# Sparse attention in eight pipelined groups of heads, and delta scan interleaved with stick attention

## The reference, cut to what matters

```python
q, k, v, g, beta = (chunk(t) for t in (q, k, v, g, beta))
...
v_new = u_c - jnp.einsum('bhcd,bhde->bhce', w_c, state)
o = jnp.einsum('bhcd,bhde->bhce', qd, state) + jnp.einsum('bhcs,bhse->bhce', qk_c, v_new)
...
log_rem = jnp.where(causal, jax.nn.log_sigmoid(-z), 0.0)
after = lax.cumsum(log_rem, axis=3, reverse=True) - log_rem
attn = jnp.where(causal, jnp.exp(jax.nn.log_sigmoid(z) + after), 0.0)
```

```python
p = _masked_softmax(logits, mask)
...
o = gates[..., 0:1] * o_cmp + gates[..., 1:2] * o_slc + gates[..., 2:3] * o_win
```

## Time and profile before

| | us |
|---|---|
| median of 3 runs | 3720.51 |
| lowest, highest | 3718.89, 3734.4 |
| profiled execution | 3725.97 |
| its span | 3724.2 |
| its mean granted TensorE clock | 0.921 |

### The profile page before, as it was taken

The page is one execution under the profiler, slowest core; times in us unless marked ns, Lnnn a source line. Parts: engine busy times, 40 slices in busy tenths (PEclk is TensorE's granted clock), DMA queues, the critical chain, the costliest instruction groups (busy, mean ns, idle before and its releaser), DMA issues. The chain is left out here.

```text
span 3724.2 us, 51371 instructions
## 1 busy us (share of the span) xinstructions
PE 3272.8 (88%) x20778; PEld 2927.4 (79%) x20778; DVE 2336.0 (63%) x2592; ACT 1543.3 (41%) x1455; POOL 186.3 (5%) x134
## 2 busy tenths in 40 slices
PE   6998699999877789999999999995489989966599
PEld 6987589999866678788788887894279989953599
DVE  7974258846742388888888885796834315434444
ACT  3432133335321177677677774441033204401243
POOL 0012000000210000000000000001600000000000
PEclk9999799989998899999999999997789969985799
DMA  7630168734201189999999996351045424520153
GB/s 314 240 113 1 46 224 325 275 125 169 80 1 68 45 297 361 343 369 364 336 365 368 367 365 260 136 184 64 0 148 187 162 68 158 184 76 0 46 181 135
DMA packets 130378, 703.20 MB, mean 189 GB/s; under 512 B 11009, under 2 KB 16145, under 8 KB 74385
## 3 DMA queue, kind: packets, MB, share of 16 engines
q1 hardware_dynamic: 118384, 650.30, 47.7%
q0 software_dynamic: 6368, 47.19, 3.2%
q10 hardware_dynamic: 5440, 3.17, 0.3%
HBM read 698.50 MB, written 1.07 MB: 188 GB/s over the span
## 5 line engine op out<-in xcount | busy, mean ns | idle before, releaser
L1048 DVE TENSOR_TENSOR ring_low<-ring,parts 128x2048 fp32r<-128x2048 f32 x570 | 1298.1, 2288 | 397.1 <-ACT parts L1911 366.0
L429 PE MATMUL banks<-parts 128*128 128x256 f32 (+1 forms) x3712 | 1170.5, 315 | 42.2 <-DVE tail_parts L1048 25.5
L430 PE MATMUL banks<-tail_parts,parts 128*128 128x256 f32 x3744 | 1062.5, 284 | 0.0
L1911 ACT ACTIVATE parts<-ring 128x2048 fp32r<-128x2048 f32 x234 | 448.4, 1917 | 876.7 <-PE banks L431 726.8
L431 PE MATMUL banks<-parts,ring_low 128*128 128x256 f32 x2816 | 798.1, 283 | 0.0
L429 PEld LDWEIGHTS banks<-parts 128*128 128x128 f32 x3712 | 708.2, 191 | 83.8 <-issue 45.6
L1978 ACT ACTIVATE parts<-ring 128x2048 fp32r<-128x2048 f32 x336 | 644.4, 1919 | 234.6 <-DMA ring<-in_wall 213.3
L430 PEld LDWEIGHTS banks<-tail_parts,parts 128*128 128x128 f32 x3744 | 712.9, 190 | 1.9 <-issue 1.9
L431 PEld LDWEIGHTS banks<-parts,ring_low 128*128 128x128 f32 x2816 | 537.8, 191 | 0.0
L430 PE MATMUL banks<-ring_low,parts 128*128 128x512 f32 x896 | 354.6, 396 | 0.0
L431 PE MATMUL banks<-parts,tail_parts 128*128 128x512 f32 x896 | 353.2, 394 | 0.0
(11 more groups left out here) (387 smaller groups left out, 3697.9 us busy)
## 6 DMA issues: line engine op xcount, KB each, us to landing
ring<-in_wall SPq DMA_DIRECT2D x616, 1024.0 KB, 6.4
big<-in_wall POOLq DMA_DIRECT2D x40, 1024.0 KB, 5.6
big<-in_w_k POOLq DMA_DIRECT2D x1, 2048.0 KB, 8.0
big<-in_w_v POOLq DMA_DIRECT2D x1, 2048.0 KB, 13.7
big<-bias_table ACTq DMA_DIRECT2D x2, 1024.0 KB, 7.4
constants<-in_con SPq DMA_DIRECT2D x1, 1377.5 KB, 7.5
x<-in_x SPq DMA_DIRECT2D x1, 1024.0 KB, 9.5
big<-big ACTq DMA_DIRECT2D x16, 64.0 KB, 2.1
```

Source lines behind the costliest of these rows:

```text
L429: pe.matmul(o, high, in_high, start=start, stop=False, **kw)
L430: pe.matmul(o, high, in_low, start=False, stop=False, **kw)
L1048: return ve.tensor_tensor(out, a, b, op)
L1911: act(parts(w_high(room, n), UNIT), ring[n % RING][:, :], ACT.Copy).then_inc(sem("w_high"), 1)
```

## The change

Delta scan and stick attention: the barriers between them go. Stick tiles get places of their own (`ZB`, `SP`, `VT`). TensorE does the scores of stick heads (`z`), the value transposes and the sums of remaining sticks (`rem`) between the steps of the delta scan; evacuations go bank by bank and head by head; the outputs are copied to SBUF (`o_out`) before they are squared; the softplus is cut into four pairs of heads; `stick` (the weighing of values) is called in `combine` behind the first unit of the up projection. Semaphores of single events are put together under `mixer`.

S5: the four products of the back rotation move from GpSimd to VectorE, behind each scan.

Sparse attention: eight groups (4 key heads x 2 branches) of four heads. Queries are normalised per block of 512 columns. Scores run two groups ahead; each head's probabilities are transposed into one of two banks (`turn`), copied out by ScalarE instead of VectorE (`turned_out`), and weighed one head later (`weigh_values`); both branches and the compressed one are summed in one PSUM bank per key head, which VectorE reads once (`o_read`). Barriers between the steps go. GpSimd's matching barriers go as well.

```diff
-        ZB, SP, VT = 0, 3072, SLOT["D"]
+        ZB, VT = CONV + 2048, HB + 1024
+        SP = (FSB, CONV + 5120, SBQ, SBQ + 768)
...
+                def z(h):
+
+                    p0 = 64 * (h % 2)
+                    j = (h // 2) * TOK
+                    o = bank[4 + h % 4]
+                    if h < 4:
+                        pe.wait_ge(*at("kvt_out", (1, 2, 7, 8)[h], l, 8))
+                    else:
+                        pe.wait_ge(*at("z_out", h - 3, l, 8))
...
+                    if h < 4:
+                        pe.wait_ge(*at("o_out", h + 1, l, 4))
+                    else:
+                        pe.wait_ge(*at("o_log", h - 3, l, 4))
+                    pe.wait_ge(*at("sp_out", h // 2 + 1, l, 4))
+                    s0 = SP[h // 2] + h % 2 * 384
+                    pe.matmul(bank[h][:, 0:TOK], con("key_after"), big(s0, TOK), start=True, stop=False)
+                    pe.matmul(bank[h][:, P:TOK], ones, big(s0 + TOK, P), start=False, stop=True)
+                    pe.matmul(bank[h][:, TOK:TOK + P], con("key_after"), big(s0 + TOK, P), start=True, stop=True)\
+                        .then_inc(sem("rem_ps"), 1)
...
+                    pe.wait_ge(*at("o_sq", b + 1, l, 4))
+                    pe.matmul(bank[4 + b][:, :], ones, big(SLOT["E"] + b * 512, 512), start=True, stop=True).then_inc(sem("o_sum"), 1)
...
+                pe.wait_ge(*at("conv_silu", 3, l, 3))
+                turn(2, 0)
+                turn(1, 0)
+                turn(1, 1)
+                pe.wait_ge(*at("level_t", 24, l, 24))
+                turn(2, 1)
+                z(0)
+                z(1)
+                pe.wait_ge(*at("kvt_out", 4, l, 8))
                 for h in range(HEADS):
...
+                    mm = pe.matmul(bank[h // 4][:, (h % 4) * P:(h % 4 + 1) * P], big(SLOT["F"] + h * P, P),
+                                   big(SLOT["D"] + h * P, P), start=True, stop=True)
+                mm.then_inc(mixer("vnew_ps", l)[0], 1)
...
+                z(2)
+                z(3)
+                pe.wait_ge(*mixer("vnew0", l))
...
+                for h in range(4, HEADS):
+                    z(h)
+                pe.wait_ge(*mixer("w_neg", l))
+                for n in range(NT):
+                    for j in range(4):
+                        mm = pe.transpose(bank[2 + n][:, j * P:(j + 1) * P], big(SBV + j * TOK + n * P, P), ident)
+                mm.then_inc(mixer("vt_ps", l)[0], 1)
...
+                rem(0)
+                pe.wait_ge(*at("z_out", 8, l, 8))
+                o_sum(0)
+                rem(1)
+                o_sum(1)
+                rem(2)
+                o_sum(2)
+                rem(3)
+                o_sum(3)
+                for h in range(4, HEADS):
+                    rem(h)
 
...
+                pe.wait_ge(*at("stick_arg", 2, l, 8))
+                pe.wait_ge(*mixer("od", l))
                 for u in range(4):
+                    if u == 1:
+                        stick(l)
+                    if u == 2:
+                        pe.wait_ge(*mixer("stick_out", l))
...
+            def logits(i):
+
+                g, br = i // 2, i % 2
+                pe.wait_ge(sem("q_normed"), g + 1)
+                for hh in range(4):
+                    h = 4 * g + hh
+                    p0 = 64 * (h % 2)
+                    if i:
+                        pe.wait_ge(sem("logits_out"), 4 * (i - 1) + hh + 1)
+                    kk = KD + br * 1024 + g * TOK
+                    pe.matmul(bank[hh][:, 0:P], qhead(h, 0), BIG[p0:p0 + 64, kk:kk + P], start=True, stop=True)
+                    pe.matmul(bank[hh][:, P:3 * P], qhead(h, 1), BIG[p0:p0 + 64, kk:kk + TOK], start=True, stop=True)\
+                        .then_inc(sem("logits_ps"), 1)
...
+                g = i // 2
+                if r > 1:
+                    pe.wait_ge(sem("pt_out"), r - 1)
+                b = bank[4 + r % 2]
+                if kind == "cmp":
+                    pe.wait_ge(*event("cmp_p"))
+                    for h in (4 * g + 2 * hh, 4 * g + 2 * hh + 1):
+                        for n in range(NT):
+                            mm = pe.transpose(b[0:NCMP, (h % 2) * TOK + n * P:(h % 2) * TOK + (n + 1) * P],
+                                              big(CP + (n * QH + h) * NCMP, NCMP), ident)
+                else:
+                    for j in range(3):
+                        mm = pe.transpose(b[:, j * P:(j + 1) * P], big(lg_at(i, hh) + j * P, P), ident)
+                mm.then_inc(sem("pt_ps"), 1)
+
+            def weigh_values(i, r, hh):
+
+                g, br = i // 2, i % 2
+                h = 4 * g + hh
+                p0 = 64 * (h % 2)
+                o = bank[6 + g % 2][p0:p0 + 64, (h // 2 % 2) * TOK:(h // 2 % 2 + 1) * TOK]
+                o1 = bank[6 + g % 2][p0:p0 + 64, (h // 2 % 2) * TOK + P:(h // 2 % 2 + 1) * TOK]
+                pe.wait_ge(sem("pt_out"), r + 1)
+                pe.matmul(o, big(VN + br * 512 + g * 64, 64), big(pt_at(i, hh), TOK), start=(br == 0 and hh < 2), stop=False,
+                          skip_group_check=True)
+                mm = pe.matmul(o1, big(VN + br * 512 + 256 + g * 64, 64), big(pt_at(i, hh) + TOK, P), start=False, stop=False,
+                               skip_group_check=True)
+                if br:
+                    mm = pe.matmul(o, BIG[0:NCMP, VC + g * 64:VC + (g + 1) * 64], big(CPT + h * TOK, TOK, 0, NCMP),
+                                   start=False, stop=True, skip_group_check=True)
+                    if hh == 3:
+                        mm.then_inc(sem("o_group"), 1)
+
+            pe.wait_ge(sem("q_out"), 4)
...
+            pe.wait_ge(*event("gate_exp"))
+            for i in range(GROUPS):
+                if i + 2 < GROUPS:
+                    logits(i + 2)
+                pe.wait_ge(sem("probs"), i + 1)
+                if i == 0:
+                    pe.wait_ge(*event("cmp_arg"))
+                if i > 3 and i % 2 == 0:
+                    pe.wait_ge(sem("o_read"), i // 2 - 1)
+                before = None
+                for r, kind, hh in turns(i):
+                    turn(i, r, kind, hh)
+                    if before is not None:
+                        weigh_values(i, *before)
+                    before = (r, hh) if kind == "head" else None
+                weigh_values(i, *before)
+            pe.wait_ge(sem("o_read"), 4)
...
+                for i, (which, b) in enumerate(((2, 0), (2, 1), (1, 0), (1, 1), (1, 2), (1, 3), (2, 2), (2, 3))):
+                    ve.wait_ge(*at("kvt", i + 1, l, 8))
+                    scale = 4 * b if which == 2 else (128 if b < 2 else 144) + 4 * b
+                    tt(chains(SLOT["C" if which == 1 else "D"] + b * 512, 4), view(bank[4 * (which - 1) + b], 0, [[P, 4], [1, P]]),
+                       view(SM, scale, [[1, 4], [0, P]]), ALU.mult).then_inc(sem("kvt_out"), 1)
...
+                for h in range(4):
+                    z_out(h)
+                ve.wait_ge(*mixer("state_ps", l))
+                ve.tensor_copy(big(ST, 512), bank[0][:, :])
+                ve.tensor_copy(big(ST + 512, 512), bank[1][:, :]).then_inc(mixer("state", l)[0], 1)
+                for h in range(4, HEADS):
...
+                sp_out(0)
+                ve.wait_ge(*mixer("vnew_ps1", l))
+                ve.tensor_copy(big(SLOT["A"] + 1024, 512), bank[4][:, :])
+                ve.tensor_copy(big(SLOT["A"] + 1536, 512), bank[5][:, :]).then_inc(mixer("vnew1", l)[0], 1)
...
+                sp_out(2)
+                sp_out(3)
+                for h in range(4):
+                    stick_arg(h)
+
+                ve.wait_ge(*mixer("o_rs", l))
+                lk(tt(big(SLOT["E"], 2048), big(SLOT["F"], 2048), big(SLOT["E"], 2048), ALU.mult))
                 ve.scalar_tensor_tensor(big(OD, 2048), big(SLOT["E"], 2048), par("dn_out_norm", 1, l), big(Z_, 2048),
...
+                ve.wait_ge(sem("scanned"), k + 1)
+                c, s = big(TC + k * 1024, 1024), big(TS + k * 1024, 1024)
+                to = rot(k)
+                tt(big(to[0], 1024), c, big(YR, 1024), ALU.mult)
+                tt(big(to[1], 1024), s, big(YI, 1024), ALU.mult)
+                if k:
+                    ve.wait_ge(sem("y_ps"), k)
+                tt(big(to[2], 1024), s, big(YR, 1024), ALU.mult)
+                tt(big(to[3], 1024), c, big(YI, 1024), ALU.mult).then_inc(sem("rotated"), 1)
...
+                                            ALU.mult, ALU.add).then_inc(sem("logits_out"), 1)
+                ve.wait_ge(sem("logits_out"), 4 * i + 4)
+                m = ROW + 8 * i
+                ve.tensor_reduce(SM[:, m:m + 4], view(BIG, lg_at(i, 0), [[384, 4], [1, P]]), AX, ALU.max)
...
+            for i in range(GROUPS):
+                if i + 2 < GROUPS:
+                    logits_out(i + 2)
+                if i == 0:
+                    ve.wait_ge(*event("cmp_exp"))
...
+                if i + 1 < GROUPS:
+                    normalise(i + 1)
+                if i % 2:
+                    g = i // 2
```

(53 more changed lines are left out.)

465 lines of the change are left out of this document (184 added, 281 removed).

## The result

| | before | after |
|---|---|---|
| median, us | 3719.7 | 3516.7 |
| ratio, 95% interval | | 0.9445, 0.9418 to 0.9473 |
| profiled execution's span, us | 3724.2 | 3514.9 |
| mean granted TensorE clock | 0.921 | 0.949 |

A later series gave 3516.59 and 0.9444 (0.9428 to 0.9460).

What follows compares the result with a forecast made beforehand. Engines working in turn, with TensorE at a low clock from short bursts, were taken to bound the changed stretches. 3726 − 96 − 8.5 − 91 = 3530.5, less 5.5 against the median: 3525 us, range 3492 to 3568.

Steps and rivals of the forecast that it cites:

- Part 1: Delta scan and stick attention, two layers: 93.6 us per layer becomes 45 to 46, gain 48 each, 96 in all.
- 40 + 2.7 + 1: Mixer, per layer: 40 us to the up projection, 2.7 for stick products at full clock, perhaps 1 of slow clock.
- Part 2: S5 back rotation on VectorE instead of GpSimd: period 17.5 us, 146.3 against 154.8 us, a gain of 8.5 us.
- upper bound of 12: S5 scan: the forecast gain was bounded between 3 and 12 us.
- The lock: S5: VectorE operations with two SBUF inputs and GpSimd reads block each other; adds return to 2.49 us, otherwise a loss of 12.
- Part 3: Sparse attention in groups: 19 us per pair, output product at 3404 instead of 3495.26, gain 91 us, bounds 67 and 106.
- The sign that I had named: Sparse attention: TensorE clock under 1 in odd groups, which were taken near half clock for half of their time.
- The rival that stood on that rule: Sparse attention: the pipeline runs but TensorE stays at 1.2 GHz; gain 67 there, kernel 3549 us; chance 0.15.
- (c): Mixer and attention: in-order queues turn overlap into hand-to-hand work; attention gains 52, mixer 30 per layer; 3600 us; chance 0.08.
- my later 22 us: Sparse attention: loss expected, before its run, from weighing each head's values directly behind its own turn; 3539 us.
- (d): Dense products behind the changed stretches: TensorE keeps 1.2 GHz there and each doubles; slower, 3740 us; chance 0.02.
- (a): All three changed places: everything at full clock and no slip, gain 218.5 us, kernel 3502 us; chance 0.20.

Runs made afterwards that it cites:

- the shared version: Changed kernel with two of the four S5 back-rotation products given back to GpSimd for every k but the last; 3528.93 us, ratio 0.9463.
- the added-turns kernel: Kernel before with 48 transposes more in each sparse-attention branch, three behind every head's value products; 3734.86 us, ratio 1.0051.

## Why the prediction was right, step by step

1. **What bounds it.** Engines working in turn, at a low clock because of it: right. The granted clock in the three changed places went from 0.74 to 0.99, and from 0.67 to 0.95; only S5 stays at 0.68, where TensorE waits for VectorE.
2. **Part 1, 96 us; measured 97.5.** The path was right: the last output sum ends 31.2 us into the stretch (forecast 31), and the normalisation behind it takes 7.5 (forecast 7.5). The sum was 38.5 us to the up projection and is 38.7; I added 1.5 for VectorE's queue, which was not needed. The scores took 3.3 us for eight heads and not 2.8; the waits on copies were 1.5 us, in one place, and not 2.3. Stick products 2.8 at full clock, as taken; the first unit took 8.6 and 9.6 us in the two layers instead of 6.9, after 4 us of idle, so the slow clock cost 1.7 to 2.7 and not 1. That the total came so close is in part luck. My terms, 40 + 2.7 + 1, make 43.7, and I wrote 45 to 46; the traces have 43.1, a gain of 50.5 us per layer and not 48. The first layer gave 5 us back ahead of the stretch, most of it that execution's own, and 7 us of the gain are the long form of the mixer in the profile of before.
3. **Part 2, 8.5 us; measured 12.8, above the upper bound of 12.** The mis-sized term is the period: 16.7 to 16.9 us, not 17.5. The four new products take 4.71 (2.36 and 2.35) and not 4.95, and handovers to itself take nothing. The lock was the step that mattered, and it held: adds 2.48 without GpSimd, and the shared version shows 6.38 for 2.35 with it. The Trainium skill, "SBUF — State Buffer", who interferes with whom, calls the pair of ports that VectorE's second SBUF input shares with GpSimd an exclusive lock, and has the order of issue decide who blocks. The runs agree. Two SBUF inputs are hit; PSUM products (4.60) and a reduction of one input (0.69) are not. In the attention GpSimd had started 0.3 us before, and VectorE alone pays (2.08 for 0.66, GpSimd 1.88 beside it as without); in S5 they take turns, and both pay (6.38 for 2.35, 3.32 for 2.34).
4. **Part 3, 91 us; measured 98.5.** The first turn came at 55.3 us (forecast 55.2) and the rest in 69 us instead of 77. Two sizes were off against each other, and that the sum is nearer than they are is luck. The clock: I took an odd group as half at 1.2 GHz, from 26 us at 0.50 of "exactly this mixture"; it was not the same mixture, for transposes stand between, and the added-turns kernel shows that in that stretch they made the difference. The sign that I had named, a clock under 1 in odd groups, did not come; the clock is 1.00 in them. The work: at full clock I had 15.5 us per pair and it is 17.7. An even group takes 6.7 us (4.6 forecast) and an odd one 10.95 (8.1): values 0.79 us a head instead of 0.48, turns 0.48 instead of 0.35, scores 1.6 instead of 1.3 per group. And VectorE's wait for the odd group (3.68 us) is not on the path, since TensorE is busy 16.6 of 17.7 us. What share of the 98.5 us belongs to the pipelining by groups, to ScalarE's copies and to the sum in PSUM was not tested; only the lag of one head was.
5. **Transposes and the clock.** The Trainium skill, "TensorE: Matmul & The Clock Gate", on transposes, has them not count towards the full clock. For fp32 transposes the runs say otherwise: added between the value products they took the clock from 0.54 to 1.00. The rival that stood on that rule, 3549 us, is out.
6. **The other rivals.** (c) hand-to-hand: TensorE turns the next head before it weighs this one, and without that the kernel takes 41 us more. The argument held, and so did the price: (c) put the attention's gain at 52 instead of 91, 39 us less. Only my later 22 us was half, since it left the clock out. (d) debt of clock: 225.5 us behind the output product against 225.8, none. (a) full clock and no slip, 3502: the clock was right, the 15.5 us under it too short.

## What to carry to other kernels

Where every engine is idle half the time, look first at the grain at which work is handed on, and at the clock that comes with it: in the mixer some 40 of 51 us per layer were left over for these, while barriers themselves were 1.4 to 1.7 us each. Before estimating a stretch by the clock of another, compare which instructions stand next to each other in both, and count a short wait per step twice, once as time and once for what it does to the clock. An idle engine is no free place for work: what GpSimd took from VectorE in the S5 scan cost more than it saved.

## What the runs showed that I had not expected

- Value products with 15 rows among them ran at 0.50 for 29 us with TensorE never idle; with 48 transposes more the stretch was as long (31.7 against 32 us) at 1.00.
- With a wait of 0.58 us per head the eight groups ran at 0.68 in the mean, whole groups of the same kind at 0.98 or at 0.50; without it at 0.99.
- The same instructions behind the same wait took 5.40 us in one execution and 3.70 in another kernel's: the clock granted over them was 0.68 and 1.00.
- Two products of VectorE (2.35 us alone) and two of GpSimd (2.34 each alone), started 0.3 us apart, took 6.7 us: about what they would take one after the other, so sharing the work bought nothing.
